# TensorE's ten middle passes of the feed-forward, written out instead of looped

## The chip, the cores and the metric

The kernel runs on one core of a Trainium2 chip. The metric is device time in microseconds. Three runs of the kernel before took 2707.13, 2697.49 and 2704.05 us (median 2704.05); the profiled execution took 2699.5 us.

Five engines run side by side, each with its own stream of instructions: TensorE (PE, matmuls; PEld are its weight loads), VectorE (DVE), ScalarE (ACT), GpSimd (POOL) and SyncE (SP), which here issues the DMAs. They meet only at semaphores.

## The reference, cut to what matters

One layer of a hybrid network on 1024 prompt rows and 8 x 16 sample rows, 1152 rows together: an input projection, a state-space branch, an attention branch, their merge, then a SwiGLU feed-forward and an embedding gate. The change is in the feed-forward:

```python
hf = rmsnorm(x, norm_ffn_g)
x = x + (jax.nn.silu(hf @ w_gate) * (hf @ w_up)) @ w_down   # 1024 -> 2816 -> 1024
```

## The kernel before, in words

All products are fp32 in three matmuls: weights and rows are split into a high and a low part, and hi x hi, hi x lo and lo x hi are summed in a PSUM bank. The 1152 rows are three blocks of 384 columns of the moving operand.

The feed-forward (`stage_ffn`) works transposed: features on partitions, rows on the free axis. Its hidden width 2816 is 22 tiles of 128. Tiles go in pairs, and a *pass* treats one pair: N = 11. In TensorE's program, `up(i, "up0", n)` is a block of 24 matmuls of line 165 (`product_block`) that makes a block of 384 rows of the gate or up projection of a pair's first tile (n = 0 to 5: three blocks of gate, three of up); `up1` does so for the second tile. `down(i)` multiplies the finished pair, act_hi and act_lo, with its rows of w_down: 24 blocks (8 output tiles x 3 row blocks) of 6 matmuls each, line 2245. The pair that `down(i)` uses was made by the pass before, so TensorE's order is

- up0 and up1 of pair 0,
- for i = 1 to 10: up0 of pair i, down of pair i-1, up1 of pair i (12 x 24 + 24 x 6 = 432 matmuls),
- down of the last pair, mixed with the first blocks of the next stage.

The ten middle passes are a hardware loop, `pe.Fori(1, N)`, on TensorE, and loops of their own on SyncE (weight loads), ScalarE and VectorE. In a loop the value that a wait compares with depends on the pass number, which is held in a register; TensorE's register instructions work these values out. `isinstance(i, int)` in `down` tells the call with a number (only the last, `down(N)`) from the calls with the loop's register.

What TensorE waits for before a block: lo_done (VectorE has made the low part of the weight tile, line 148, after ScalarE has made the high part, line 139), acc_read_v (VectorE has read what the bank held six blocks ago: line 2376 or 2387 after an up, line 2418, the sum into x, after a down), and before the first block of a down f_steps (`steps.sem`: VectorE has made the three pieces of act_lo, line 2397, from act_hi, ScalarE's line 2321). Weight tiles go through two slots, w_hi0/w_lo0 and w_hi1/w_lo1; banks 0 to 5 are used in turn.

The engine's instructions lie in memory and come to it by DMA; the trace shows these transfers as queues of kind "instruction".

Of the kernel before, what the change touches and what calls it, by code (L numbers as in the profile page):

```python
# [150 lines left out]
def product_block(S, pe, slot, acc, rhs, rb, ready, free, kts=KT, more=None, before=None):  # L151

    if ready is not None:
        pe.wait_ge(S.lo_done, ready)
    pe.wait_ge(*free)
    hi = S.w_hi[slot][:, 0:kts * P].rearrange("p (k c) -> p k c", k=kts)
    lo = S.w_lo[slot][:, 0:kts * P].rearrange("p (k c) -> p k c", k=kts)
    a_hi, a_lo = rhs
    rows = slice(rb * RBN, (rb + 1) * RBN)
    n = 0  # L160
    for k in range(kts):
        if before is not None:
            before(k)
        for w, a in ((hi, a_hi), (hi, a_lo), (lo, a_hi)):
            last = pe.matmul(acc[:, 0:RBN], w[:, k, :], a[:, k, rows],  # L165
                             start=(n == 0), stop=(n == 3 * kts - 1 and more is None))
            n += 1
    if more is not None:
        last = more()
    last.then_inc(S.acc_done, 1)  # L170
# [1647 lines left out]
def rb_cols(rb):  # L1818
    return slice(rb * RBN, (rb + 1) * RBN)
# [328 lines left out]
def stage_ffn(nc, S, A, ctx, own, b0, bv0, u0, next_tiles):  # L2148


    N = FT // 2
# [27 lines left out]
    def blk(i, part, n):  # L2179

        if isinstance(i, int) and i == 0:
            return {"up0": 0, "up1": 6}[part] + n
        return 12 + 36 * (i - 1) + {"up0": 0, "down": 6, "up1": 30}[part] + n
# [4 lines left out]
    def slot(part, n):  # L2188
        return ({"up0": 0, "down": 6, "up1": 30}[part] + n) % 6
# [26 lines left out]
    def tensor(pe, first_gate, first_emb_block):  # L2216
        def up(i, part, n, before=None):
            b = blk(i, part, n)

            t = (0 if part == "up0" else 2) + n // 3 if isinstance(i, int) and i == 0 else \  # L2220
                4 + 6 * (i - 1) + (0 if part == "up0" else 4) + n // 3
            par = ((0 if part == "up0" else 2) + n // 3) % 2
            product_block(S, pe, (u0 + par) % 2, acc[slot(part, n)], (S.R0_hi, S.R0_lo), n % 3,
                          HEAD + u0 + t + 1, (S.acc_read_v, HEAD + bv0 + b - 5), before=before)

        def down(i):

            for n in range(24):
                d, rb = n // 3, n % 3
                half = d // 4  # L2230

                final = isinstance(i, int)
                b = blk(i, "down", n) - (6 if final else 0)
                pe.wait_ge(S.lo_done, HEAD + u0 + 4 + 6 * (i - 1) + (0 if final else 2) + half + 1)
                if n == 0:
                    pe.wait_ge(steps.sem, low_value(i))
                pe.wait_ge(S.acc_read_v, HEAD + bv0 + b - (2 if final and n >= 15 else 5))
                s = (u0 + half) % 2
                wh = S.w_hi[s][:, :].rearrange("p (k c) -> p k c", k=2)
                wl = S.w_lo[s][:, :].rearrange("p (k c) -> p k c", k=2)  # L2240
                m = 0
                a = acc[n % 3 if final and n >= 12 else slot("down", n)]
                for k in range(2):
                    for w, r in ((wh, act_hi), (wh, act_lo), (wl, act_hi)):
                        last = pe.matmul(a[:, 0:RBN], w[:, k, (d % 4) * P:(d % 4 + 1) * P],  # L2245
                                         r[:, k, rb_cols(rb)], start=(m == 0), stop=(m == 5))
                        m += 1
                last.then_inc(S.acc_done, 1)
                if final and n >= 12 and rb == 2:
                    first_gate(pe, 2 * (d - 4), acc[3:6], HEAD + bv0 + blk(N, "down", 9) - 6)  # L2250
                    if d == KT - 1:
                        first_emb_block(pe, 0)
                        first_emb_block(pe, 1)
                    first_gate(pe, 2 * (d - 4) + 1, acc[3:6], HEAD + bv0 + blk(N, "down", 9) - 6)

        def turn_p(m):
            pe.wait_ge(p_in, 32)
            if m >= 2:
                pe.wait_ge(plo_done, m - 1)
            else:  # L2260
                pe.wait_ge(var_done, 3)
            for r in range(3):
                last = pe.transpose(sums[m % 2][:, r * P:(r + 1) * P],  # L2263
                                    p_rows[:, 3 * (m // 2) + r, (m % 2) * P:(m % 2 + 1) * P], S.ident[:, :])
            last.then_inc(pt_done, 1)

        def low_value(i):

            return F_FIRST + F_PASS * (i - 1)

        def sum_up(rb):
            if rb == 0:
                pe.wait_ge(S.x_squares, START + 3 * KT)
            if rb == 2:
                pe.wait_ge(var_done, 1)
            pe.matmul(sums[rb % 2][:, 0:RBN], S.ones[:, :], S.ss[:, rb_cols(rb)], start=True, stop=True)\  # L2276
              .then_inc(sum_done, 1)

        pe.wait_ge(S.hf_split, START + 3 * (KT - 2))
        for n in range(6):  # L2280

            def split_in(k):
                if n < 3 and k >= KT - 2:
                    pe.wait_ge(S.hf_split, START + 3 * k + n + 1)
            up(0, "up0", n, split_in)
            if n == 2:
                sum_up(0)
                sum_up(1)
            if n == 3:
                sum_up(2)  # L2290
        turn_p(0)
        turn_p(1)
        for n in range(6):
            up(0, "up1", n)
            if n < 2:
                turn_p(2 * n + 2)
                turn_p(2 * n + 3)
        with pe.Fori(1, N) as i:
            for n in range(6):
                up(i, "up0", n)  # L2300
            down(i)
            for n in range(6):
                up(i, "up1", n)
        down(N)

    def scalar(act):
# [171 lines left out]
    def gpsimd(pool):  # L2478

        for n in range(24):  # L2480
# [4 lines left out]
            else:  # L2485
                pool.wait_ge(ss_done, n - 2)
                pool.tensor_tensor(S.ss[:, rb_cols(rb)], S.ss[:, rb_cols(rb)], squares[n % 6][:, :], ALU.add)\
                    .then_inc(ss_done, 1)

    return Engines(sync, tensor, scalar, vector, gpsimd)  # L2490


# [464 lines left out]
```

## Time and profile before

| | |
|---|---|
| runs | 2707.13, 2697.49, 2704.05 us |
| profiled execution | 2699.5 us |
| its span, first to last instruction | 2697.8 us |
| TensorE busy | 2615.7 us, 97% |
| VectorE busy | 1528.2 us, 57% |
| ScalarE busy | 836.3 us, 31% |
| mean granted TensorE clock | 0.984 of full speed |
| instruction transfers | q8: 105 packets, 1.72 MB; q14: 80 packets, 0.66 MB |

The span is the profiled execution without what lies before the first and after the last instruction, 1.7 us. Matmuls are pipelined: the row of one shows how long it took from start to its modelled end, while the next has already begun, so the pace is read from a count over a stretch, not from one row. Register, branch and semaphore instructions are not counted as busy.

### The profile page before, as it was taken

The page shows a single profiled execution, that of the slowest core. Times are in us where ns is not written, and L with a number is a line of the kernel's source. Part 1 is how long each engine was busy: PE and PEld are TensorE (multiplying, and loading weights), DVE is VectorE, ACT ScalarE, POOL GpSimd, SP SyncE. Part 2 cuts the span into 40 slices and gives each one's busy share as a digit, 9 for nine tenths or more (in the row PEclk, how much of TensorE's full clock was granted, in tenths as well). Part 3 has the DMA queues.
Part 4 walks back from the last instruction along what each step waited for, and adds up shares of the span by engine and source line. Part 5 has one row for each costly group of instructions (what it writes and reads, how often), then busy time and mean ns, then how long its engine had stood idle before and what let it go on. Part 6 is the DMA issues. An engine that isn't in the chain of part 4 may idle for free. (4 is left out here: it accounts for less than half of the span.)

```text
span 2697.8 us, 47913 instructions
## 1 busy us (share of the span) xinstructions
PE 2615.7 (97%) x17088; PEld 2491.2 (92%) x17088; DVE 1528.2 (57%) x2585; ACT 836.3 (31%) x1564; POOL 345.4 (13%) x327
## 2 busy tenths in 40 slices
PE   6999999999999999999979999999999999999897
PEld 6888888888879999999979999999999999999897
DVE  4666766666675757575753443545444444444754
ACT  4443434344342425343431222211111111111513
POOL 0222322322231011111100002000000000000300
PEclk8999999999999999999979999999999999999999
DMA  5444544456524141436255433411111111111112
GB/s 137 92 109 75 120 82 100 91 82 106 84 69 71 25 103 28 101 33 101 33 197 189 162 102 126 144 40 46 40 39 47 39 46 40 39 47 39 36 41 80
DMA packets 331857, 214.35 MB, mean 79 GB/s; under 512 B 117828, under 2 KB 312216, under 8 KB 331672
## 3 DMA queue, kind: packets, MB, share of 16 engines
q1 hardware_dynamic: 331672, 211.98, 33.1%
q8 instruction: 105, 1.72, 0.3%
q14 instruction: 80, 0.66, 0.1%
HBM read 164.51 MB, written 47.41 MB: 79 GB/s over the span
## 5 line engine op out<-in xcount | busy, mean ns | idle before, releaser
L165 PE MATMUL bank<-operand_hi,w_hi 128*128 128x384 f32 x1584 | 533.6, 337 | 1.5 <-DVE w_lo L148 1.5
L165 PE MATMUL bank<-operand_hi,w_lo 128*128 128x384 f32 x1584 | 530.7, 335 | 0.0
L165 PE MATMUL bank<-operand_lo,w_hi 128*128 128x384 f32 x1584 | 530.5, 335 | 0.0
L139 ACT ACTIVATE w_hi<-w_raw 128x1024 fp32r<-128x1024 f32 (+1 forms) x167 | 172.6, 1034 | 779.5 <-PE bank L165 485.8
L165 PEld LDWEIGHTS bank<-operand_hi,w_hi 128*128 128x128 f32 x1584 | 298.1, 188 | 2.1 <-issue 1.8
L165 PEld LDWEIGHTS bank<-operand_lo,w_hi 128*128 128x128 f32 x1584 | 298.0, 188 | 0.3
L165 PEld LDWEIGHTS bank<-operand_hi,w_lo 128*128 128x128 f32 x1584 | 297.8, 188 | 0.0
L694 PE MATMUL acc<-operand_hi,w_hi 128*128 128x384 f32 x792 | 281.3, 355 | 5.5 <-PEq L215 5.5
L1153 POOL TENSOR_TENSOR wgt<-wgt,left 128x128 f32<-128x128 f32 (+2 forms) x224 | 209.8, 942 | 580.6 <-DVE left L1105 411.6
L165 PE MATMUL sacc<-operand_hi,w_hi 128*128 128x384 f32 x768 | 266.5, 347 | 6.1 <-DVE w_lo L148 3.3
L148 DVE TENSOR_TENSOR w_lo<-w_raw,w_hi 128x1024 fp32r<-128x1024 f32 (+1 forms) x167 | 201.6, 1208 | 119.7 <-ACT w_hi L139 118.6
L694 PE MATMUL acc<-operand_hi,w_lo 128*128 128x384 f32 x792 | 267.4, 338 | 0.0
L694 PE MATMUL acc<-operand_lo,w_hi 128*128 128x384 f32 x792 | 266.7, 337 | 0.0
L1105 DVE TENSOR_TENSOR_SCAN left<-keep,left 128x128 f32<-128x128 f32 (+2 forms) x224 | 241.7, 1092 | 43.2 <-ACT keep L941 40.9
L165 PE MATMUL sacc<-operand_hi,w_lo 128*128 128x384 f32 x768 | 258.5, 337 | 0.0
L165 PE MATMUL sacc<-operand_lo,w_hi 128*128 128x384 f32 x768 | 258.4, 337 | 0.0
L2418 DVE TENSOR_TENSOR x_t<-x_t,bank 128x384 f32<-128x384 f32 x264 | 142.4, 552 | 91.8 <-PE bank L2245 91.8
L941 ACT ACTIVATE keep<-z 128x128 f32<-128x128 f32 (+2 forms) x224 | 108.9, 486 | 243.9 <-PE z L749 109.2
L2245 PE MATMUL bank<-f_act_hi,w_hi 128*128 128x384 f32 x528 | 178.7, 338 | 3.9 <-issue 3.9
L2245 PE MATMUL bank<-f_act_lo,w_hi 128*128 128x384 f32 x528 | 178.6, 338 | 0.0
L2245 PE MATMUL bank<-f_act_hi,w_lo 128*128 128x384 f32 x528 | 178.5, 338 | 0.0
L1040 DVE COPY w_t<-tp 128x128 f32<-128x128 f32 (+2 forms) x224 | 113.4, 541 | 99.5 <-PE tp L773 98.2
(357 smaller groups left out, 4454.5 us busy)
## 6 DMA issues: line engine op xcount, KB each, us to landing
w_raw<-in_w_in SPq DMA_DIRECT2D x65, 512.0 KB, 8.0
k_cache<-in_cache_k SPq DMA_DIRECT2D x256, 64.0 KB, 2.5
v_cache<-in_cache_v SPq DMA_DIRECT2D x64, 256.0 KB, 4.3
w_raw<-in_w_gate SPq DMA_DIRECT2D x22, 512.0 KB, 3.7
w_raw<-in_w_up SPq DMA_DIRECT2D x22, 512.0 KB, 3.8
w_raw<-in_w_down SPq DMA_DIRECT2D x22, 512.0 KB, 3.8
s_gate_a<-gate SPq DMA_DIRECT2D x24, 192.0 KB, 2.8
s_o<-o_t SPq DMA_DIRECT2D x8, 576.0 KB, 9.1
```

What stands on the lines that cost most here:

```text
L139: act.activation(hi, S.raw[u0 % 2][:, 0:cols], ACT.Copy).then_inc(S.hi_done, 1)
L148: dve.tensor_tensor(lo, S.raw[u0 % 2][:, 0:cols], hi.bitcast(F32), ALU.subtract).then_inc(S.lo_done, 1)
L165: last = pe.matmul(acc[:, 0:RBN], w[:, k, :], a[:, k, rows], start=(n == 0), stop=(n == 3 * kts - 1 and more is None))
L694: last = pe.matmul(a[:, 0:RBN], w[:, k, :], x[:, k, rows], start=(k == 0 and n == 0), stop=(k == KT - 1 and n == 2))
L941: act.activation(keep[u % 2][:, 0:n], zb[u % 2][:, 0:n], ACT.Sigmoid, scale=-SB_SCALE)\
L1040: dve.tensor_copy(w_t[x % 4][:, 0:c, :], src[:, 0:c * P].rearrange("p (c m) -> p c m", c=c))\
L1105: dve.tensor_tensor_scan(rev(lf, c0, c1), rev(k, 0, n), rev(k, 0, n), lf[:, c1:c1 + 1], ALU.mult, ALU.bypass).then_inc(S.p_done, 1)
L1153: pool.tensor_tensor(w[:, 0:n], w[:, 0:n], left[left_of(u)][:, c0 + 1:c1 + 1], ALU.mult)\
L2245: last = pe.matmul(a[:, 0:RBN], w[:, k, (d % 4) * P:(d % 4 + 1) * P], r[:, k, rb_cols(rb)], start=(m == 0), stop=(m == 5))
L2418: ins = dve.tensor_tensor(x[:, d, rb_cols(rb)], x[:, d, rb_cols(rb)], acc[n % 3 if final and n >= 12 else slot("down", n)][:, 0:RBN], ALU.add)
```

## The change

TensorE's loop over the ten middle passes becomes a Python loop, so that the ten passes stand in its program one after the other; the pass number is then a Python number, and the test for the last pass in `down` asks for it by value. The other engines keep their loops, and their instructions are the same.

```diff
-                final = isinstance(i, int)
+                final = isinstance(i, int) and i == N
@@
-        with pe.Fori(1, N) as i:
+        for i in range(1, N):
             for n in range(6):
                 up(i, "up0", n)
             down(i)
             for n in range(6):
                 up(i, "up1", n)
         down(N)
```

TensorE's program before, where the loop begins (operand0 are the rows, bank0 the block of pass 1, up0):

```order
L165 MATMUL bank5<-operand0_hi,w_lo0 128x384
L2298 UNCONDITIONAL_BRANCH
L2298 ISA
L155 ISA [waits w_lo_done]
L165 MATMUL bank0<-operand0_hi,w_hi1 128x384 [waits acc_read_v]
L165 MATMUL bank0<-operand0_lo,w_hi1 128x384
```

and at the first block of its down, for which f_act are the finished pair:

```order
L165 MATMUL bank5<-operand0_hi,w_lo0 128x384
L2234 REGISTER_ALU
L2236 ISA [waits w_lo_done]
L2237 REGISTER_ALU [waits f_steps]
L2245 MATMUL bank0<-f_act_hi,w_hi1 128x384 [waits acc_read_v]
L2245 MATMUL bank0<-f_act_lo,w_hi1 128x384
```

and where the loop ends, ahead of the down of the last pair:

```order
L165 MATMUL bank5<-operand0_hi,w_lo0 128x384
L2298 REGISTER_ALU
L2298 COMPARE_AND_BRANCH
L2245 MATMUL bank0<-f_act_hi,w_hi1 128x384 [waits acc_read_v,f_steps,w_lo_done]
L2245 MATMUL bank0<-f_act_lo,w_hi1 128x384
```

A register instruction in the loop carries one of a block's waits, the matmul the other; in the down of the last pair, outside the loop, all stand before the matmul.

TensorE's program now, at the first block of the down in the first of the ten passes:

```order
L165 MATMUL bank5<-operand0_hi,w_lo0 128x384
L2245 MATMUL bank0<-f_act_hi,w_hi1 128x384 [waits acc_read_v,f_steps,w_lo_done]
L2245 MATMUL bank0<-f_act_lo,w_hi1 128x384
L2245 MATMUL bank0<-f_act_hi,w_lo1 128x384
```

and at the seam between the first and the second pass:

```order
L165 MATMUL bank5<-operand0_lo,w_hi0 128x384
L165 MATMUL bank5<-operand0_hi,w_lo0 128x384
L165 MATMUL bank0<-operand0_hi,w_hi1 128x384 [waits acc_read_v,w_lo_done]
L165 MATMUL bank0<-operand0_lo,w_hi1 128x384
```

The branches and the register instructions are gone, the 432 matmuls of a pass follow one another ten times, and each block's first matmul has the waits before it with constant values, in the form that the last down had already.

## Rows read from the trace of the kernel before

**Rows 1.** Page: busy us (share of the span) and instructions; instruction queue: packets, MB, share.
```profile
PE 2615.7 (97%) x17088; PEld 2491.2 (92%) x17088; DVE 1528.2 (57%) x2585; ACT 836.3 (31%) x1564; POOL 345.4 (13%) x327
...
q8 instruction: 105, 1.72, 0.3%
```

**Rows 2.** Chain of waits through the middle passes: start us, us, what.
```profile
1783.27 24.97 PE bank L2245 x144
1808.24 49.95 PE bank L165 x288
...
2482.52 25.00 PE bank L165 x144
...
2511.37 18.48 PE bank L2245 x90
```

**Rows 3.** Windows (us; busy by engine; clock; DMA): passes 1, 2, 10; eleventh down.
```profile
1758.30:1833.20 74.90, 74.90 (x434) 74.90 (x433) 35.74 (x60) 11.34 (x18) 0.00 (x0) 1.00 0.14 43
1833.20:1908.10 74.90, 74.90 (x434) 74.90 (x433) 35.68 (x60) 11.33 (x18) 0.00 (x0) 1.00 0.14 42
2432.50:2507.40 74.90, 74.90 (x433) 74.69 (x431) 35.69 (x60) 11.34 (x18) 0.00 (x0) 1.00 0.14 42
2517.30:2529.60 12.30, 12.30 (x73) 12.23 (x71) 11.71 (x18) 8.22 (x17) 7.21 (x8) 1.00 0.20 54
```

**Rows 4.** Line 2245, middle passes: ns min/median/max, first and last start us.
```profile
L2245 PEld LDWEIGHTS bank<-f_act_hi,w_hi x480: 187/188/188, 1782.9 to 2481.7; 128*128 128x128 f32 x160
L2245 PE MATMUL bank<-f_act_hi,w_hi x480: 332/336/338, 1783.1 to 2481.8; 128*128 128x384 f32 x160
...
L2245 PE MATMUL bank<-f_act_lo,w_hi x480: 336/336/339, 1783.3 to 2482.0; 128*128 128x384 f32 x160
```

**Rows 5.** Timeline where the loop ends: start us, us, what [idle before <-releaser].
```profile
2507.55 1.06 ACT L139 ACTIVATE w_hi<-w_raw 128x1024 fp32r<-128x1024 f32 x1 [10.18 <-PE bank L165]
2507.55 0.56 DVE L2387 TENSOR_TENSOR f_hid<-bank,f_rstd 128x384 f32<-128x384 f32 x1 [2.54 <-PE bank L165]
...
2509.78 1.49 DVE L2397 TENSOR_TENSOR f_act_lo<-f_hid,f_act_hi 128x384 fp32r<-128x384 f32 x3
...
2511.37 0.66 PE L2245 MATMUL bank<-f_act_hi,w_hi 128*128 128x384 f32 x1 [3.86 <-issue]
...
2511.82 0.52 PE L2245 MATMUL bank<-f_act_lo,w_hi 128*128 128x384 f32 x1
```

**Rows 6.** VectorE's waits, 1758 to 2507.5: us, times, longest.
```profile
DVE x_t L2418 <- PE bank L2245: 86.8, 180, 0.5
```

**Rows 7.** Timeline of VectorE at the start of the first down.
```profile
1784.40 1.23 DVE L148 TENSOR_TENSOR w_lo<-w_raw,w_hi 128x1024 fp32r<-128x1024 f32 x1
1785.54 1.48 DVE L2418 TENSOR_TENSOR x_t<-x_t,bank 128x384 f32<-128x384 f32 x3
```

**Rows 8.** Waits of the weight loads, whole span: us, times, longest.
```profile
PEld acc L694 <- issue: 11.0, 63, 0.2
```

**Rows 9.** DMA queues, 1758.3 to 1833.2 (first pass): packets, MB, share.
```profile
q8 instruction: 4, 0.07, 0.4%
```

**Rows 10.** DMA queues, 1833.2 to 2507.5 (nine passes): all queues that moved anything.
```profile
DMA packets 41568, 28.32 MB, mean 42 GB/s; under 512 B 864, under 2 KB 36704, under 8 KB 41568
...
q1 hardware_dynamic: 41568, 28.32, 14.0%
```

**Rows 11.** DMA queues, 150 to 1120 (attention stage).
```profile
q1 hardware_dynamic: 166706, 77.73, 42.2%
q8 instruction: 67, 1.10, 0.5%
```

**Rows 12.** Waits, 255 to 275 (an attention loop starts over).
```profile
PEld z L743 <- issue: 1.2, 1, 1.2
PE z L743 <- issue: 0.8, 1, 0.8
```

**Rows 13.** DMA queues, 255 to 275.
```profile
q8 instruction: 3, 0.05, 0.9%
```

## The prediction

> **What bounds the kernel now.** Start with the page's busy times [rows 1]: TensorE is busy for 2615.7 of 2697.8 us, so only what TensorE does, or waits for, can move the end. Next the chain of waits through the feed-forward [rows 2]: from 1783.27 to 2507.52 us it holds TensorE pieces alone, 24.97 or 24.98 us for 144 matmuls of line 2245 (a down projection) and then 49.95 us for 288 of line 165 (up1 of that pass and up0 of the next), each piece starting where the last ended. Both give 49.95 / 288 = 24.97 / 144 = 0.1734 us per matmul. One pass is 24.97 + 49.95 = 74.92 us, and ten passes, from about 1758.3 to 2507.5 us, are 749.2 us. The windows [rows 3] say the same of single passes: 74.90 of 74.90 us busy in the first, the second and the last, with the granted clock at 1.00, the upper of the two levels (2.4 GHz). Last, every matmul alone [rows 4]: the 480 of each kind in line 2245 have a median of 336 ns and a longest of 338 or 339 (each overlaps its successor, which is why 336 ns long ones follow each other every 173), and their weight loads are 187 to 188 ns without an exception. A reader should see that inside the loop there is no idle time to win. What the loop's branch costs the instruction stream is hidden already.
>
> **The change part by part.**
>
> *Work.* Each middle pass keeps its 432 matmuls with the same tiles and banks, and the other four engines have the same instructions as before. 432 x 0.1734 = 74.9 us per pass before and after: 0.
>
> *The branch and the register arithmetic.* The loop's branch, its counter and the sums for the wait values go. They run in TensorE's instruction stream ahead of the array. The eight seams between passes that the chain shows lie inside the 49.95 us pieces [rows 2], and such a piece has the same 0.1734 us per matmul as a piece without a seam. So the branches, nine jumps back in all, cost 0 now and give 0 back.
>
> *Leaving the loop.* The one gap nearby is 3.86 us before the first matmul of the eleventh down, and the trace writes "issue" beside it, which could be read as the price of falling out of the loop. The rows of that stretch say otherwise [rows 5]: VectorE makes the last three pieces of act_lo from 2509.78 for 1.49 us, so until 2511.27, and the matmul starts at 2511.37; its first wait is for exactly these (f_steps). In front of them stand the reads of the last up1 bank at 2507.55, w_hi, w_lo and act_hi. This chain is data, and no part of it changes: 0. The clock drop that follows it stays too: the first two matmuls take 0.66 and 0.52 us, and 90 matmuls from 2511.37 take 18.48 us, against 90 x 0.1734 = 15.6.
>
> *Waits.* In the loop one of a block's two waits stands on a register instruction ahead of the matmul and the other on the matmul; afterwards both stand before it with constant values, which puts a wait in the instruction stream ahead of each block, as now. That form can be seen running in the kernel before, in the first half of the eleventh down, which is written without a loop: from 2517.30 to 2529.60 us TensorE is busy for 12.30 of 12.30 us [rows 3]. The values waited for are early: VectorE waits for TensorE 180 times in the middle passes, 86.8 us in all, so 0.48 us each [rows 6], and a sum takes it about 0.5 us [rows 7]; a bank is thus free about a microsecond after its block, and TensorE asks for it five blocks later, 5 x 6 x 0.1734 = 5.2 us. The weights are as early: ScalarE stands idle for 10.18 us until TensorE frees a slot [rows 5], and then splits it in 1.06 us. The worst place is the start of a down, where a 1.23 us weight split delays VectorE, and its first three sums run back to back from 1785.54, the first of them 2.27 us after the down began at 1783.27 [rows 7]; 5.2 us still cover that. Below: 0. Above: the nearest rows with short stops of the instruction stream before weight loads are those of line 694 in the attention stage, 11.0 us over 63 stops, 0.17 us each [rows 8]; on all 360 blocks of the ten passes that would be 63 us. I take 0, since the rows of the eleventh down show this very form.
>
> *Code that has to arrive.* This is the new cost to weigh. The packets of queue q8 are instruction transfers, 105 of them with 1.72 MB [rows 1], so 16 KB each. Through the first pass, whose code arrives while it runs, there are 4 of them [rows 9]; from 1833.2 to 2507.5 us, through nine passes, none at all [rows 10]: the body stays in the buffer. Written out, each of those nine passes brings its own code, at most 9 x 4 = 36 packets in 674 us, one per 19 us or slower. Is a packet paid for? The first pass is the control in the trace: with 4 packets it takes what the second takes without any, 74.90 us busy of 74.90 [rows 3]. The attention stage also brings its code all the time: 67 packets between 150 and 1120 us, one per 14.5 us, with the data queue at 42.2% there against 14.0% in the nine passes [rows 10, 11]. So more code per microsecond arrives there, in a fuller queue. The new packets add 36 x 16 KB = 0.6 MB to the 28.32 MB of data in that stretch, and a weight tile that lands a little later is covered by ScalarE's 10 us. Below: 0, the first pass. Above: at 255 to 275 us, where a loop of the attention stage starts over and three packets come in 20 us [rows 13], TensorE stops once for 0.8 us (its weight loads for 1.2) for no reason but "issue" [rows 12]; on every packet that is 36 x 0.8 = 29 us, or 43 by the weight loads. I take 0: the first pass is the same code on the same engine.
>
> One rule speaks about this place. The Trainium skill ("Runtime: NRT & Kernel Launch", Instruction fetch mechanics) says that the sequencer streams straight code on its own, with block crossings mostly hidden, but that a taken branch whose target is not in the buffer stalls for a fetch, so that written-out code is to be preferred. By the first half the sum stays 0, and the trace agrees: 4 packets in the first pass and no idle time. The second half would be a gain of 9 jumps back; the trace disagrees for this loop, with 0 packets over nine passes.
>
> **The sum** is 0 + 0 + 0 + 0 + 0 against the profiled execution's 2699.5 us (span 2697.8). The median of the runs is 2704.05, 4.5 us above it; since nothing is taken off or added, I predict that median, 2704 us.
>
> **Rivals.**
>
> 1. *Code arrives too late.* Place: the boundary of each 16 KB piece in passes two to ten; price 0.8 us each; it decides as soon as the buffer, over a straight run of 750 us, falls behind by one packet. 36 x 0.8 = 29 us: 2733 us, slower (43 us: 2747). For it: the stops where an attention loop starts over. Against it: the first pass, and 67 packets in a busier stage. 8 in 100.
> 2. *Waits shorten the run ahead.* A wait for a bank ahead of every block keeps the instruction stream from running far enough ahead; 360 x 0.17 = 63 us: 2767 us. For it: the stops at line 694. Against it: the first half of the eleventh down runs without a gap. 3 in 100.
> 3. *The loop was not free.* The gap at its end is partly branch and code after all: at most 3.86 us and the 18.48 - 15.6 = 2.9 us of clock, 6.8 us: 2697 us. If each of 9 jumps back also cost 0.8 us, another 7.2: 2690 us. For it: the word "issue" beside the gap. Against it: act_lo ends 0.10 us before the matmul, and the seams show nothing. 5 in 100, about half of it over the bound of 0.3%.
> 4. *The passes are not the same passes.* The test for the last pass is changed too, and a middle pass taken for the last would mix the final stage's gate blocks into its down. The order of instructions has none there, so the change would be one in words only: 2704 us, as forecast. 1 in 100.
>
> **How the numbers follow.** The forecast has 83 in 100, and with it about 2 in 100 on either side for runs that spread: the three of before lie between 2697.49 and 2707.13, so 0.3%, 8 us, is about what a measurement can tell. Faster: half of rival 3 and 2, about 5 in 100; slower: rivals 1 and 2 and 2, 13; the same: 82. The likeliest's own range is 2696 to 2712; I draw it out to 2691 on the side of rival 3 and to 2722 on the side of rival 1, as far as a packet price of half a microsecond (18 us). Rivals 1 and 2 at full price are left outside.
>
> **What would show it.** In the profile after: the passes again 74.9 us each with the granted clock at 1.00, no idle time of TensorE between 1758 and 2507 us, the 3.9 us gap before the eleventh down unchanged, and about 32 to 36 more 16 KB packets in the code queue, spread evenly. Wrong would be a weight load of line 165 or 2245 that starts late at a regular distance of about 20 us (rival 1), or at the start of most blocks (rival 2), or a shorter gap at 2507 (rival 3).

## The result, and the profile after

The changed kernel takes 2710.54 us (median of nine runs, 2707.08 to 2715.97); nine runs of the kernel before have a median of 2703.77 (2697.49 to 2707.13). The ratio is 1.0033 [1.0023, 1.0043]: slower by a third of a per cent, where no change was forecast. The profiled execution took 2711.4 us (span 2709.7), so 11.9 us more span than that of before.

The first question is whether the ten passes became longer. The page's busy line and code queue of the kernel after, beside [rows 1]:

```profile
PE 2623.1 (97%) x17088; PEld 2498.9 (92%) x17088; DVE 1528.5 (56%) x2585; ACT 836.2 (31%) x1564; POOL 345.4 (13%) x327
...
q8 instruction: 137, 2.24, 0.3%
```

The same instructions, and 32 more packets of code. The chain of waits of the kernel after through the passes (start us, us, what), beside [rows 2]:

```profile
1795.40 24.98 PE bank L2245 x144
1820.38 49.95 PE bank L165 x288
1870.32 24.98 PE bank L2245 x144
...
2419.73 49.95 PE bank L165 x288
2469.68 24.98 PE bank L2245 x144
2494.65 25.00 PE bank L165 x144
...
2523.50 18.37 PE bank L2245 x90
```

and windows of the kernel after over its first, second and tenth pass (columns as in [rows 3]):

```profile
1770.42:1845.32 74.90, 74.90 (x434) 74.90 (x433) 35.71 (x60) 11.33 (x18) 0.00 (x0) 1.00 0.14 43
1845.32:1920.22 74.90, 74.90 (x434) 74.90 (x433) 35.66 (x60) 11.33 (x18) 0.00 (x0) 1.00 0.14 43
2444.66:2519.56 74.90, 74.90 (x433) 74.66 (x431) 35.66 (x60) 11.34 (x18) 0.00 (x0) 1.00 0.13 43
```

Every pass takes what it took. But the first down starts at 1795.40 us where it started at 1783.27 [rows 2], and the last begins at 2523.50 against 2511.37: 12.13 us late at the start of the passes and 12.13 us late at their end. The time was lost before TensorE came to the changed code. To find the place, the start of the same weight load of TensorE in both traces, counted by its number, is subtracted:

| start in the trace of before, us | after minus before, us |
|---|---|
| 266.8 | +1.4 |
| 768.5 | +1.4 |
| 824.0 | +6.4 |
| 836.6 | +8.9 |
| 1081.9 | +7.4 |
| 1127.9 | +11.8 |
| 1290.5 | +11.3 |
| 1961.6 | +12.1 |

The largest step is at 824 us, where the attention stage ends and the state-space stage begins (*the seam* from here on, not to be mixed up with the seams between passes). The waits of TensorE there, of the kernel after (us, times, longest; the first line has no counterpart before):

```profile
PE stp L1429 <- DMA hist<-in_state_conv: 4.7, 1, 4.7
PE o L794 <- ACT o_t L955: 0.7, 1, 0.7
```

Line 1429 turns around the convolution's history (`hist`), which SyncE loads. SyncE's timeline at the seam, of the kernel before (start us, us, what it issues):

```profile
810.44 0.39 SPq L130 DMA_DIRECT2D w_raw<-in_w_in  x1
810.93 0.53 SPq L682 DMA_DIRECT2D s_o<-o_t  x1
820.79 1.16 SPq L1251 DMA_DIRECT2D hist<-in_state_conv  x3
```

and of the kernel after:

```profile
811.79 0.39 SPq L130 DMA_DIRECT2D w_raw<-in_w_in  x1
812.28 0.53 SPq L682 DMA_DIRECT2D s_o<-o_t  x1
827.87 1.16 SPq L1251 DMA_DIRECT2D hist<-in_state_conv  x3
```

The order is the same; the third step comes 7.08 us later, of which 1.35 us are the earlier offset. Between the second and third stands VectorE, which clears `hist` once the last store of the attention stage (`s_o`, 576 KB) has landed. VectorE's timeline of the kernel before:

```profile
820.14 0.07 DVE L1720 MEMSET stream<- 128x12 f32 x1 [9.73 <-DMA s_o<-o_t]
```

and of the kernel after:

```profile
827.22 0.07 DVE L1720 MEMSET stream<- 128x12 f32 x1 [15.45 <-DMA s_o<-o_t]
```

From issue to landing that store took 8.9 us before and 14.6 after, and the load of a w_in tile issued 0.49 us ahead of it took 8.0 and 13.7. So a 512 KB load that has nothing to do with the change became 5.7 us slower; the store behind it landed 5.7 us later, then VectorE's clearing and the `hist` load followed, and TensorE stood still for 4.7 us (about a microsecond of the 5.7 had been to spare). TensorE's timeline of the kernel after:

```profile
825.34 0.34 PE L165 MATMUL sacc<-operand_hi,w_lo 128*128 128x384 f32 x1
830.39 0.88 PE L1429 MATMUL stp<-ident,hist 128*128 128x128 f32 x3 [4.72 <-DMA hist<-in_state_conv]
```

The idle time has a tail. Windows of TensorE at the seam (us; length, busy; clock; DMA; GB/s), of the kernel before:

```profile
825.00:829.00 4.00, 4.00 (x25) 1.00 1.03 227
829.00:836.00 7.00, 7.00 (x42) 1.00 0.30 41
```

and of the kernel after:

```profile
825.00:829.00 4.00, 0.67 (x4) 1.00 0.27 102
829.00:836.00 7.00, 5.61 (x19) 0.51 0.88 203
836.00:846.00 10.00, 10.00 (x59) 1.00 0.21 19
```

The granted clock falls while TensorE still waits and is at the lower of its two levels (1.2 GHz) from 829.15 to 835.98 us, 6.8 us in all; in the window from 829 to 836 us it reads 0.51. The seam thus costs 5.0 us of waiting and 2.5 of clock, the steps +1.4, +6.4, +8.9 of the table. The rest of the 11.9 us, +4.4 between 1082 and 1128 us above all, is clock drops at other places; single executions differ there by as much (experiment 2), so it is not put down to the change.

### The profile page after: what moved, and what is told of

Read it like the earlier page. It is cut to its first block and busy times, and to the rows that moved or that the text cites. A ratio compares the mean times of both kernels' runs of the same rounds, so it can differ in the third digit from the quotient of the medians.

```text
span 2709.7 us, 47822 instructions
## 1 busy us (share of the span) xinstructions
PE 2623.1 (97%) x17088; PEld 2498.9 (92%) x17088; DVE 1528.5 (56%) x2585; ACT 836.2 (31%) x1564; POOL 345.4 (13%) x327
```

## The experiments

Their question: why is an unrelated load slower? Theories, with the letters of the first four expectations: (A) the difference is chance, of one build or one chip; (B) the longer program itself slows the earlier stages, because certain loads become slower and one of them sits at the seam; (C) the passes or their code cost time after all. All ratios are against the kernel before, run on the same chip.

**1. The changed kernel again** (no edit).

> The kernel after once more, not a line changed. Its first profile has the middle passes at 74.92 us each, as before, and loses 12 us ahead of them, most of it (5 us of idle time and the clock drops after it) between 815 and 1140 us, where the program is the same. Theory A (chance: memory transfers of the earlier stages happen to be slow in one execution and not in another): a ratio to before of 1.000 within 0.002, and in the new profile the passes begin within 4 us of 1758. Theory B (the longer program itself slows the earlier stages, through where things lie or arrive): a ratio of 1.002 to 1.004 again, and the passes begin 5 to 12 us later than 1758 while each takes 74.9 us. Theory C (code arriving during the passes stops TensorE in most executions, only not in the one profiled): a ratio of 1.002 to 1.004, and passes longer than 75.5 us in the new profile.

Measured: 1.0036 [1.0022, 1.005], median 2711.35 (six runs). TensorE waits 4.9 us for `hist`, VectorE 15.6 us for `s_o`. It repeats with fresh runs of both kernels: not A, chance.

**2. The test alone**, with the loop kept.

```diff
-                final = isinstance(i, int)
+                final = isinstance(i, int) and i == N
```

> The kernel before with only the test for the last pass changed, the loop kept: the same instructions on every engine, so a control of how far two builds of one program differ. A, B and C alike: a ratio of 1.000 within 0.001. Anything beyond 0.002 means that a difference of the size measured for the change needs no cause in it.

Measured: 1.0000 [0.999, 1.001], 2701.31 us. TensorE has no wait for `hist` there. Its profile also serves as a ruler: the same instructions in an execution with a median of no difference start from 2.7 us earlier to 5.2 us later than in the profile of before, by clock drops in the state-space stage. So single profiles tell the seam's 7.5 us from nothing, but not the last 4 us.

**3. Code that never runs.** The loop stays as before; behind TensorE's last instruction stands a jump over 4045 matmuls, so that the program is about as long as the changed one.

```diff
                     end.tensor(pe)
+                    skip = pe.alloc_register("skip")
+                    pe.reg_mov(skip, 0)
+                    with pe.If_ne(skip, 0):
+                        for _ in range(4045):
+                            pe.matmul(S.bank[0][:, 0:RBN], S.w_hi[0][:, 0:P], S.R0_hi[:, 0, 0:RBN], start=True, stop=True)
```

> The kernel before with its loop, and behind TensorE's last instruction a jump over 4045 matmuls that are never run: TensorE's program is as long as the one written out, but nothing of it is fetched or run in the passes. A: 1.000 within 0.002. B: 1.002 to 1.004 (2709 to 2714 us), the passes beginning 5 to 12 us late. C: 1.000 within 0.001. The jump at the end, beside the last stores, costs at most 2 us in all three.

Measured: 1.0046 [1.0028, 1.0064], 2710.43 us (six runs). The code queue of its page and TensorE's timeline at the seam:

```profile
q8 instruction: 107, 1.75, 0.3%
```

```profile
829.23 1.09 PE L1429 MATMUL stp<-ident,hist 128*128 128x128 f32 x4 [4.44 <-DMA hist<-in_state_conv]
```

Nothing of the passes is written out, only two more packets are fetched, and the loss is all there, with the same wait. This rules out C for the loss and shows that code which never runs brings it.

**4. Half written out**: a loop of two rounds of five passes each.

```diff
-        with pe.Fori(1, N) as i:
-            ...
+        with pe.Fori(0, 2) as o:
+            for j in range(5):
+                middle(5 * o + j + 1)
```

> The ten passes as a loop of two rounds with five passes written out in each: the program grows by four passes instead of nine, but five passes are more than the buffer was seen to keep, so that the code of nearly all ten passes has to arrive during them (about 30 more 16 KB packets than before). A: 1.000 within 0.002. B: four ninths of the difference, 1.001 to 1.002 (2706 to 2708 us). C: the whole difference, 1.002 to 1.004, or more by what the one jump back costs (0.8 us at the attention loop).

Measured: 1.0007 [0.9996, 1.0018], 2702.75 us. It fetches 139 packets, two more than the changed kernel, and no loss is measured: the second half against C. For B four ninths of the loss were expected, 1.001 to 1.002; the interval [0.9996, 1.0018] can't tell that from 1. Its chain of waits shows the one jump back, in the middle:

```profile
2104.01 24.99 PE bank L165 x144
2128.99 0.55 issue
2129.54 25.23 PE bank L165 x144
```

Here a jump does cost something: 0.55 us of idle time and about 0.25 in the piece behind it. The body of five passes does not stay as the single pass does: it is fetched again for the second round, where the kernel before takes 0 packets in nine passes [rows 10].

**5 to 8. What moves the slow loads?** A tile is a block of 128 columns of w_in. In every trace ten to twelve of the 65 w_in tiles take 11 us or more to land: the first two of all, the eight blocks of one class (1024 columns apart, not counting the 16 columns of dt; the dt tile joins them in experiments 4 and 12), and up to three others. The class is the same in the traces of before and of experiments 2 and 6, and the same in those of the changed kernel and of experiments 1, 3, 5 and 8. Landing of single tiles from issue, us, by the traces (those of the late class in bold; dead is experiment 3, twice_five 4, after_longer 13, dead_longest 14):

| first column (note) | before | twice_five | after | dead | after_longer | dead_longest |
|---|---|---|---|---|---|---|
| 5008 | **13.2** | 9.7 | 8.1 | 8.0 | 6.4 | 5.8 |
| 896 | **12.5** | 10.4 | 8.8 | 8.9 | 6.7 | 6.5 |
| 1024 | 10.6 | **14.8** | 9.6 | 9.8 | 10.5 | 9.5 |
| 128 | 6.7 | 7.9 | **12.4** | **12.7** | 8.1 | 8.3 |
| 1152 (the seam) | 8.0 | 9.5 | **13.7** | **13.3** | 9.7 | 9.7 |
| 1280 | 5.3 | 7.6 | 7.9 | 7.8 | **12.3** | **12.3** |
| 2304 | 5.3 | 7.6 | 7.9 | 8.0 | **12.3** | **12.2** |

The late block wanders by 128 columns (512 bytes of a row) from 896 to 1024 to 1152 to 1280 as the program grows by 0, about 2000, about 4000 and about 6000 matmuls. Before has eight late tiles too; they are issued at 581, 601, 644, 694, 1180, 1221, 1255 and 1281 us, where TensorE waits for no weights.

Experiments 5 and 6 lengthen a scratch array instead of the program, in the changed kernel by 1024 bytes and in the kernel before by 3072:

```diff
-            return nc.dram_tensor(name, (KT, P, ROWS), F32).ap()
+            n = KT * P * ROWS
+            return nc.dram_tensor(name, (n + (256 if name == "s_gate_a" else 0),), F32).ap()[0:n] ...
```

> The kernel after, with 1024 bytes more behind one scratch array in HBM (s_gate_a), which nothing reads or writes; the instructions are the same. In the profiles so far a w_in weight tile loads in 5 to 9 us or, for about one column block of 128 in eight, in about 12 us; which ones is the same in every execution of one program, and differs by program: columns 896 and 2944 of w_in and 3984, 5008, 6032, 7056 in the kernel before (so 896 or, past the 16 columns of dt, 912 more than a multiple of 1024), 128, 1152, 2176, 7312 and 5264, 6288 after (128 or 144 more). One of those after, column 1152, is loaded just ahead of the state-space stage. Theory P (the program's length moves where w_in lies, by 1024 bytes against 4096 from before to after): if the scratch array moves w_in as well, the slow tiles are those of before again and the ratio is 1.000 within 0.002; if it doesn't, they are those of after and the ratio is 1.003 to 1.005. Theory L (the length costs by itself, wherever the arrays lie): 1.003 to 1.005 with whichever tiles.

> The kernel before, loop kept, with 3072 bytes more behind the same scratch array. P: if scratch moves w_in, the slow tiles are those of the kernel after (columns 128 and 1152 among them) and the ratio is 1.003 to 1.005 with no change in any instruction; if it doesn't, 1.000 and the tiles of before. L: 1.000 within 0.001.

Measured: 1.0030 [1.0015, 1.0045] (2711.43 us) and 1.0004 [0.9989, 1.0018] (2703.08). The late tiles are those of the kernel changed in each case, so 1024 or 3072 bytes more of scratch memory move nothing; larger steps were not tried. Experiment 8 makes the dead code eight matmuls longer (4053):

> The kernel before with the jump over dead code as in the run before, the dead code longer by 8 matmuls (1024 bytes, if each is a weight load and a matmul of 64 bytes). P, if arrays follow the program byte by byte: the slow tiles are two column blocks further and the ratio changes from 1.0046, to about 1.000 if they are those of before. P, if the program takes its place in larger steps: tiles and ratio as with the shorter dead code, 1.003 to 1.006. L: 1.003 to 1.006.

Measured: 1.0033 [1.0019, 1.0048], 2709.76 us; the tiles of after, a wait of 5.0 us for `hist`. So a step of some 1000 bytes of program moves nothing either.

Experiment 7 issues the `s_o` store ahead of the tile at the seam, in the changed kernel:

```diff
-                        if m % 3 == 2:
+                        if m % 3 == 2 and not (t.last and m // 3 == 1):
                             weight(t, m // 3)
...
                 sp.dma_start(S.d_o[ds(t.i, 1)]..., o_t[:, :]).then_inc(o_stored, 16)
+                if t.last:
+                    weight(t, 1)
```

> The kernel after, and at the end of the attention stage SyncE issues the store of s_o ahead of the load of the w_in tile at column 1152 instead of behind it. In the profile after, that load takes 18.3 us (12.6 before), the store behind it 14.6 us (9.1 before), VectorE waits for the store 15.5 us (9.7), TensorE idles 5 us at line 1429 and its clock falls. If that chain is what the 7 to 9 us are made of: the store lands within 9 us, TensorE idles under 2 us at line 1429, and the ratio falls to 1.000 to 1.002. If it is not: 1.003 to 1.005.

Measured: 1.0033 [1.0016, 1.005], 2709.31 us: no gain. (The 18.3 and 12.6 us of the expectation run from the tile's issue to that of the next w_in load; from issue to landing it is 13.7 and 8.0.) TensorE's waits from 600 to 1300 us in this run:

```profile
PE sacc L165 <- issue: 4.5, 1, 4.5
...
PE sacc L165 <- DVE w_lo L148: 3.6, 1, 3.6
PE stp L1431 <- DMA hist<-in_state_conv: 2.2, 1, 2.2
```

and in the kernel before:

```profile
PE sacc L165 <- DVE w_lo L148: 3.3, 1, 3.3
PE sacc L165 <- issue: 2.8, 1, 2.8
```

The two waits of line 165 are not at the seam: they stand at 994 and 1140 us, and the kernel before has both, at 988 and 1128. What the new order changed is that the store, now first, lands in 2.9 us, and that `hist` is issued 13.3 us earlier. But the late tile now stands ahead of `hist`: issued at 812.50 us, it lands after 15.2 us, at 827.7, and TensorE, which waits 2.2 us for `hist`, goes on at 828.58. In this trace the seam still costs 5.6 us (against the kernel before, counted as in the table, from +0.4 us at 768 to +6.0 at 837), so this order was no test of a seam without the loss.

**9 and 10. Both ahead of the tile**: the `s_o` store and the `hist` loads are issued, then the tile; in the changed kernel (9) and in the kernel before (10).

```diff
-                        if m % 3 == 2:
+                        if m % 3 == 2 and not (t.last and m // 3 == 1):
...
+                if t.last:
+                    S.seam_load = lambda: weight(t, 1)
...
             load_hist(0)
+            S.seam_load()
             load_h0(0)
```

> The kernel after; between the attention and the state-space stage SyncE issues the store of s_o and the three loads of hist ahead of the load of the w_in tile at column 1152, which comes before them in the kernel after. The run with only the store ahead still had TensorE wait 2.2 us for hist and once 4.5 us more, and its clock low more often later, and measured 1.0033. Theory S (the seam: the slow tile delays the store and hist, TensorE idles, the clock falls): no wait for hist at line 1429 over 1 us, the offset against the kernel before at the start of the state-space stage under 4 us instead of 9, ratio 1.000 to 1.002. Rival N (the slow tiles cost all along the state-space stage, not at the seam): the wait is gone and the ratio stays at 1.003 to 1.004.

> The same new order of these DMAs in the kernel before, with its loop. There the tile at column 1152 is a fast one and TensorE does not wait for hist. S: 0.999 to 1.000 (up to 3 us where the store and hist come earlier). N: 1.000 within 0.001.

Measured: 1.0016 [1.0004, 1.0028] (2705.5 us) and 1.0001 [0.999, 1.0012] (2702.37). SyncE's timeline in experiment 9:

```profile
812.47 0.38 SPq L682 DMA_DIRECT2D s_o<-o_t  x1
816.35 1.16 SPq L1253 DMA_DIRECT2D hist<-in_state_conv  x3
817.55 0.40 SPq L130 DMA_DIRECT2D w_raw<-in_w_in  x1
```

`hist` is issued 11.5 us earlier, the wait for it is gone, TensorE is busy without a gap from 815 to 846 us at a clock of 1.00, and about half of the loss is back. In the kernel before the same order gives nothing, so it is no win of its own. (Both wait twice for later tiles, 5.9 and 6.2 us in all; so does the kernel before, 3.3 and 2.8 us.)

**11. A stand-in for the late tile, in the kernel before**: a copy of w_in's columns 1152 to 1279 to scratch memory, which no one uses, ahead of the `s_o` store.

```diff
+                if t.last:
+                    sp.dma_start(S.d_decoy.rearrange("(r c) -> r c", c=P), A.w_in[0][:, 1152:1152 + P]).then_inc(S.decoy, 16)
                 sp.dma_start(S.d_o[ds(t.i, 1)]..., o_t[:, :]).then_inc(o_stored, 16)
... (the scratch array, and SyncE's wait for the copy at the end of the state-space stage)
```

> The kernel before with its loop; ahead of the store of s_o SyncE also issues a copy of the 1024 x 128 block of w_in at column 1152 to a scratch array that nobody reads, so that the store and hist stand behind more packets, as they do behind the slow tile in the kernel after. The program is as short as before and its fast and slow tiles should be those of before. S: the store lands 4 to 12 us later than 9.1, TensorE waits 3 to 10 us for hist at line 1429 and its clock falls there, ratio 1.002 to 1.005. N: the wait appears too, but the ratio stays under 1.002.

Measured: 1.0038 [1.0026, 1.0051], 2708.74 us (ten runs). SyncE's timeline and TensorE's:

```profile
811.10 0.39 SPq L130 DMA_DIRECT2D w_raw<-in_w_in  x1
811.59 0.60 SPq L683 DMA_DIRECT2D s_decoy<-in_w_in  x1
812.23 2.88 SPq L684 DMA_DIRECT2D s_o<-o_t  x1
828.02 1.16 SPq L1253 DMA_DIRECT2D hist<-in_state_conv  x3
```

```profile
830.55 1.09 PE L1432 MATMUL stp<-ident,hist 128*128 128x128 f32 x4 [5.57 <-DMA hist<-in_state_conv]
```

The store lands after 14.8 us (14.6 in the changed kernel), `hist` is issued within 0.2 us of where the changed kernel issues it, and the kernel with its loop becomes as slow as the one without. A late store at the seam is enough for the whole loss.

**12 to 14. Other lengths.** If it is the late class and not length as such, the loss goes away when the program is made shorter or still longer. Experiment 12 has 2022 dead matmuls behind the kernel before, 13 has them behind the changed kernel, 14 has 6067 behind the kernel before; the edit is that of experiment 3 with another count.

> The kernel before with the jump over 2022 dead matmuls instead of 4045, so that TensorE's program is about as long as that of the two rounds of five passes. P (slow tiles go by the program's length): the slow tiles are those of the two rounds of five (columns 1024, 2048, 7184 and the dt tile), others than with 4045, and the ratio is 1.000 to 1.002 as there. If a longer program costs by length whichever tiles are slow: half of the 4045's, 1.0015 to 1.0025, with any tiles.

> The kernel after, passes written out, and behind TensorE's last instruction a jump over 2022 dead matmuls: longer than the kernel after by as much as the half-length dead code. From the kernel before each such step has moved the slow tiles by one block of 128 columns: 896, then 0, then 128. P: the next step moves them to 256 (columns 256, 1280, 2304 and, past dt, 3344, 4368, 5392, 6416, 7440), none of which is loaded at the seam; the wait for hist at line 1429 is under 1 us and the ratio 1.000 to 1.001, faster than the kernel after although the program is longer. Cost by length: 1.004 to 1.006. Something in the written-out passes themselves: 1.003 to 1.004.

> The kernel before with its loop and a jump over 6067 dead matmuls, as long as the run beside it, with nothing written out. P: the same slow tiles at 256 and so on, and 1.000 to 1.001. Cost by length: 1.005 to 1.007. The difference between this run and the one beside it is what the written-out passes cost or give in themselves: 0 within 0.001 by all that the profiles show of the passes.

Measured: 1.0003 [0.9993, 1.0013] (2700.03 us), 1.0007 [0.9994, 1.002] (2702.11) and 1.0013 [0.9998, 1.0028] (2703.46). The waits for `hist` are 0.6, 0.8 and 0.7 us, VectorE's for `s_o` 11.3, 11.5 and 11.4. Experiment 14 lies a little above its forecast of 1.000 to 1.001, but its interval includes 1. Experiment 13 is the strongest of the study: the ten passes are written out as in the changed kernel, 2022 matmuls that never run are added, and the loss is not there any more.

| program | matmuls more than before | late block | ratio |
|---|---|---|---|
| test alone (2) | 0 | 896 | 1.0000 |
| two times five (4) | 1728, run | 1024 | 1.0007 |
| dead half (12) | 2022, dead | 1024 | 1.0003 |
| changed kernel | 3888, run | 1152 | 1.0033 |
| dead (3) | 4045, dead | 1152 | 1.0046 |
| dead longer (8) | 4053, dead | 1152 | 1.0033 |
| changed and longer (13) | 3888 run, 2022 dead | 1280 | 1.0007 |
| dead longest (14) | 6067, dead | 1280 | 1.0013 |

What stays open: why a block of columns is late at all. That the length of the program decides where w_in comes to lie is the plain reading, but no address stands in the trace, and only the rule of the table was shown. Open too is the rest of experiment 9, 0.16%: its interval and that of experiment 10 overlap. By their traces it is not at the seam or behind it: 9 runs 2.8 us behind 10 at 768 us and still 2.8 us at 1758. In the seven traces with the late class of the changed kernel TensorE is 0.4 to 2.3 us late at 768 us against the kernel before, in the four others with the class of before it is between 0.6 early and 0.7 late; what makes that was not tested. None of these kernels is faster than the kernel before.

## Why the prediction was wrong, point by point

**Work, 0:** right. A pass takes 74.92 us before and after.

**Branch and register arithmetic, 0:** right for this loop; the seams between passes are as long as before. (The chain has nine of the 49.95 us pieces, one for each jump back, not eight; nothing hangs on it.) Experiment 4 shows what decides it: with a body of five passes the one jump back costs 0.55 us of idle time, close to the 0.8 us where an attention loop starts over [rows 12]. The rule on taken branches in the Trainium skill ("Runtime: NRT & Kernel Launch", Instruction fetch mechanics), weighed in the prediction, agrees with experiment 4; the loop before, which fetches nothing [rows 10], shows no such stall.

**Leaving the loop, 0:** right. The timeline of the kernel after at that place, beside [rows 5]:

```profile
2521.91 1.49 DVE L2397 TENSOR_TENSOR f_act_lo<-f_hid,f_act_hi 128x384 fp32r<-128x384 f32 x3
...
2523.50 0.66 PE L2245 MATMUL bank<-f_act_hi,w_hi 128*128 128x384 f32 x1 [3.86 <-issue]
```

The gap is 3.86 us as before, although there is no loop left to leave: it was data, as read.

**Waits, 0:** right. VectorE's wait for a down's bank is unchanged, of the kernel after, beside [rows 6]:

```profile
DVE x_t L2418 <- PE bank L2245: 86.9, 180, 0.5
```

**Code that has to arrive, 0:** right in number and price. DMA queues of the kernel after from its second pass to its tenth (packets, MB, share), beside [rows 10]:

```profile
q1 hardware_dynamic: 41568, 28.32, 13.8%
q8 instruction: 31, 0.51, 0.3%
```

At most 36 packets were reckoned; 31 came in these nine passes, one per 22 us, and experiments 3 and 4 separate their price from the loss: without them 1.0046, with them 1.0007 [0.9996, 1.0018].

**The sum, 0: this step failed.** It holds five terms, all of the stretch from 1758 us on, and ends with "nothing is taken off or added". That says that all that lies before the changed code stays as it is because its instructions stay. The chip showed otherwise: a program longer by some 4000 matmuls, run or never run, has other late tiles, one of them at a seam with a microsecond to spare, and the missing term is +5.0 us of waiting and +2.5 of clock at 824 to 837 us in the profiled execution. The difference of the medians is 6.8 us (9.2 to 10.1 in experiments 1, 3 and 5, each over its own runs of before). Whether the term appears hangs on the length: in four programs of other lengths (experiments 4 and 12 to 14) the median differs by at most 0.13%, and each interval includes 1.

**The rivals.** Rival 1 (code too late, 2733 us) and rival 2 (shorter run ahead, 2767 us) were the only mechanisms on the slower side, and neither came about: no weight load of line 165 or 2245 starts late in the passes. Rival 3 is refuted by the unchanged gap. Rival 4 did not come about either: the passes have the same matmuls, and the new test by itself (experiment 2) changes nothing. The true course was on nobody's list. The time, 2710.54 us, lies inside the range and inside the likeliest's own 2696 to 2712, but that is luck: the range was drawn for the spread of runs and for rivals that did not happen. As a measured change of 0.33% it belongs to the side that was given 13 in 100, and for other reasons.

## What to carry to other kernels

An edit that changes a program's length can move time in a stage that it does not touch; look for where the offset between two traces begins before looking at the edited lines. Where a change is worth less than half a per cent, run the old kernel with dead code of the same length as a control: it tells the edit's own worth from that of the length. And look in the profile for seams where one late transfer holds up a chain of store, clearing and load with little to spare; here a decoy of 512 KB alone cost the kernel before a third of a per cent.

## What the runs showed of the hardware that was not expected

- Loads of the same shape differ by program: the tiles of the table above land in 5.3 to 10.6 us in some programs and in 12.2 to 14.8 in others, and in each program eight of the 65, 1024 columns apart, are the late ones.
- Which ones depends on the program's length: some 2000 matmuls of TensorE code, about 270 KB (an estimate: 32 more packets of 16 KB for 9 x 432 matmuls are 135 bytes each), move the late block by 128 columns; some 1000 bytes of code and 1024 or 3072 bytes of scratch do not. The cause is open.
- A loop body of one pass, 432 matmuls, runs nine more times without a packet; one of five passes pays 0.55 us at its jump back.
- In the pause at the seam (4.7 us by the matmuls, 5.0 by the weight loads) the granted clock fell to its lower level, for 6.8 us, which added 2.5 us to the pause; in experiment 11 more of the same 6.8 us lay inside the pause (5.6 us by the matmuls), and they added 1.7.
- A 576 KB store landed in 2.9 us when it was issued ahead of a 512 KB load (experiments 7, 9 and 10), in 8.9 us behind a fast one (before) and in 14.6 us behind a late one (after).
